# One weight array and one product of 448 columns for the second layer's queries and rotary keys

## The reference, cut to what matters

```python
def shared_kv(x, pos, kv_norm, kv_w_down, kv_latent_norm):
    h = rmsnorm(x, kv_norm)
    lat = h @ kv_w_down                     # 1024 -> 256 + 64
    ckv = rmsnorm(lat[..., :KV_LORA], kv_latent_norm)
    krope = rope(lat[..., KV_LORA:], pos)   # the rotary keys, 64 columns
    return ckv, krope
def mla_layer(x, k, v, pos, q_offset, norm_pre, w_in, q_norm, w_uq, w_out, norm_post):
    h = rmsnorm(x, norm_pre)
    proj = h @ w_in                         # 1024 -> 384 + 1024
    q_lat, gate = proj[..., :Q_LORA], proj[..., Q_LORA:]
    q = (rmsnorm(q_lat, q_norm) @ w_uq).reshape(B, T, H_B, NOPE + ROPE)
    ...
```

## Time and profile before

| | us |
|---|---|
| median of 3 runs | 659.3 |
| the runs | 660.23, 659.3, 653.32 |
| the profiled execution, its own time | 654.99 |
| its span, first to last instruction | 653.2 |
| PE busy | 619.9 (95%) |
| DVE busy | 401.2 (61%) |
| ACT busy | 297.5 (46%) |
| POOL busy | 123.7 (19%) |

### The profile page before, as it was taken

How to read it: one execution, slowest core, us unless ns; L and a number is a source line. 1 busy time by engine, 2 the same in 40 slices (tenths; PEclk the granted TensorE clock), 3 DMA queues, 4 the chain that set the end, 5 groups by cost and what they waited for, 6 DMA issues and landing times.

```text
span 653.2 us, 12063 instructions
## 1 busy us (share of the span) xinstructions
PE 619.9 (95%) x4702; PEld 598.4 (92%) x4702; DVE 401.2 (61%) x612; ACT 297.5 (46%) x578; POOL 123.7 (19%) x140
## 2 busy tenths in 40 slices
PE   5999999999999899997999999999999979989996
PEld 5989999999999799997999999988999978789996
DVE  5475755564564792258657767467788776664414
ACT  7785623432532352246323422365556667753311
POOL 0200200100030152236325400210000126630002
PEclk9999999999999899999999999999999999989999
DMA  8932280261262263232243410331111126766004
GB/s 317 332 108 65 64 259 18 66 204 55 74 193 66 73 228 112 83 112 98 67 113 84 129 65 2 112 85 30 34 29 38 49 81 199 236 214 255 1 1 162
DMA packets 66280, 73.68 MB, mean 113 GB/s; under 512 B 8112, under 2 KB 58544, under 8 KB 66096
## 3 DMA queue, kind: packets, MB, share of 16 engines
q1 hardware_dynamic: 66224, 72.91, 35.5%
HBM read 62.12 MB, written 10.78 MB: 112 GB/s over the span
## 4 chain that ended last, share of the span: by engine, by line
PE 64%; DVE 15%; ACT 11%; issue 4%; POOL 3%; DMA 3%; DVEq 0%; ACTq 0%; POOLq 0%
PE bank L1477 21%; PE bank L1479 20%; PE bank L1478 20%; DVE slab_lo L1175 2%; ACT prob L1109 2%; ACT slab_hi L922 2%; DVE pT_lo L1175 2%; DMA stage<-in_cache_ckv_dram 1%; DVE rows L1393 1%; DVE prob L1445 1%; DMA stage<-in_b_w_out_dram 1%; DVE qN_lo L1175 1%; DVE hat_lo L1175 1%; POOL skL L902 1%; POOL cn_lo L898 1%
## 5 line engine op out<-in xcount | busy, mean ns | idle before, releaser
L1477 PE MATMUL bank<-slab_hi,hat_hi 128*128 128x256 f32 (+2 forms) x600 | 171.8, 286 | 11.8 <-DVE slab_lo L1175 8.3
L1478 PE MATMUL bank<-slab_lo,hat_hi 128*128 128x256 f32 (+2 forms) x600 | 170.6, 284 | 0.0
L1479 PE MATMUL bank<-slab_hi,hat_lo 128*128 128x256 f32 (+2 forms) x600 | 170.5, 284 | 0.0
L1477 PEld LDWEIGHTS bank<-slab_hi,hat_hi 128*128 128x128 f32 x600 | 115.9, 193 | 12.7 <-DVE slab_lo L1175 8.5
L1478 PEld LDWEIGHTS bank<-slab_lo,hat_hi 128*128 128x128 f32 x600 | 116.0, 193 | 0.0
L1479 PEld LDWEIGHTS bank<-slab_hi,hat_lo 128*128 128x128 f32 x600 | 116.0, 193 | 0.0
L1175 DVE TENSOR_TENSOR slab_lo<-stage,slab_hi 128x1024 fp32r<-128x1024 f32 (+3 forms) x70 | 84.3, 1205 | 18.0 <-ACT slab_hi L922 16.0
L1477 PE MATMUL bank<-hat_hi,slab_hi 128*128 128x320 f32 x256 | 80.6, 315 | 0.6 <-DVE rows L1401 0.4
L1478 PE MATMUL bank<-hat_lo,slab_hi 128*128 128x320 f32 x256 | 79.8, 312 | 0.0
L1479 PE MATMUL bank<-hat_hi,slab_lo 128*128 128x320 f32 x256 | 79.7, 311 | 0.0
L922 ACT ACTIVATE slab_hi<-stage 128x1024 fp32r<-128x1024 f32 (+3 forms) x70 | 71.0, 1014 | 14.2 <-POOL stage L857 6.0
(11 more groups left out here) (334 smaller groups left out, 1440.5 us busy)
## 6 DMA issues: line engine op xcount, KB each, us to landing
stage<-in_a_w_in_dram SPq DMA_DIRECT2D x22, 512.0 KB, 5.1
stage<-in_b_w_in_dram SPq DMA_DIRECT2D x10, 512.0 KB, 4.2
st_s<-in_state_gla_dram SPq DMA_DIRECT2D x4, 1024.0 KB, 7.0
out_dram<-st_s SPq DMA_DIRECT2D x4, 1024.0 KB, 5.3
stage<-in_a_w_out_dram SPq DMA_DIRECT2D x8, 512.0 KB, 4.6
stage<-in_ckvT_dram SPq DMA_DIRECT2D x8, 512.0 KB, 3.5
stage<-in_cache_ckv_dram SPq DMA_DIRECT2D x8, 512.0 KB, 4.1
stage<-in_b_w_out_dram SPq DMA_DIRECT2D x8, 512.0 KB, 3.9
```

Source lines behind the costliest of these rows:

```text
L1477: pe.matmul(out, a[0], b[0], start=first, stop=False)
L1478: pe.matmul(out, a[0], b[1], start=False, stop=False)
L1479: return pe.matmul(out, a[1], b[0], start=False, stop=last)
```

## The change

`ql0` and `kq` become one weight `krq` of 448 columns (64 rotary, then 384 query). It has four pieces of two k-steps each, 896 elements a partition, in a slab of its own (slab 4), which lies where the second layer's latents and keys come later. Two pieces are loaded where `ql0` was, two where `kq` was. The products are one step for each tile, `("krq", t)`: 24 matmuls of 448 columns into one bank. PE waits before k-steps 0, 2, 4 and 6 of tile 0 for the pieces 0, 1, 2 and 3. DVE copies 64 and 384 columns out of each bank, and one step `kr` rotates the keys of all five tiles from the copy `kr_raw`. The other weights' alternation between slabs 0 and 1 leaves `krq` out.

```diff
-    out["ql0"] = halves("b_w_in", 0, "b_norm_pre")
-    out["kq"] = [[("kv_w_down", k, k + 4, KL, ROPE, "kv_norm"), ("b_w_in", k, k + 4, 256, QL - 256, "b_norm_pre")] for k in (0, 4)]
+    out["krq"] = [[("kv_w_down", k, k + 2, KL, ROPE, "kv_norm"), ("b_w_in", k, k + 2, 0, QL, "b_norm_pre")] for k in range(0, KD, 2)]
...
-SLAB_NO = {name: n for n, name in enumerate(SLABS)}
+SLAB_NO = {name: n for n, name in enumerate(name for name in SLABS if name != "krq")}
...
-            load("ql0")
+            out += [("piece", "krq", j) for j in range(2)]
...
 def latent_layer(out, load):
     out += [("lcn",)]
-    load("kq")
-    out += [("qa",), ("qas",)]
+    out += [("piece", "krq", j) for j in range(2, KD // 2)]
+    out += [("krq", t) for t in range(2)]
     load(("gb", 3))
-    out += [("kq",), ("kqs",), ("cn",), ("och",), ("qs",)]
+    out += [("krq", t) for t in range(2, NT)] + [("kr",), ("cn",), ("och",), ("qs",)]
...
         place[0] = qlT_at
+        slab[4] = pair("slab4", [P, KD * KRQ])
+        assert place[0] <= temp_at
+        kr_raw = thb[:, NT * ROPE:].rearrange("p (t n) -> p t n", n=ROPE)
+        place[0] = qlT_at
...
                 elif kind == "qs":
-                    after(pool, "act", "kqs")
+                    after(pool, "act", "krq", NT - 1)
                     s, r = S1(("qa",)), S1(("qa",), stat2)
-                    link(pool.tensor_tensor(r, s, S1(("qb",)), ADD))
-                    link(pool.tensor_scalar(r, r, 1.0 / QL, EPS, MUL, ADD))
+                    link(pool.tensor_scalar(r, s, 1.0 / QL, EPS, MUL, ADD))
...
+                    if name == "krq" and j == 0:
+                        after(act, "pe", "o", HA - 1)
+                        after(act, "dve", "gl", NT - 1)
+                        act.wait_ge(state_out, 16 * HA)
+                        act.wait_ge(final_out, 16 * HA)
...
+                elif kind == "krq":
+                    last = act.activation(junk[:, 0:QL], bank[:, 0, ROPE:KRQ], ACT.Square, accum_out=S1(("qa",), t=step[1]))
...
-                    if kind[0] == "q":
-                        last = dve.tensor_copy(qln[:, t, 0:256], v)
-                    else:
-                        link(rotate(krn[:, t, :], v[:, :, 0:ROPE],
-                                    [cst(c).rearrange("p (t n) -> p t n", n=RH)[:, t, :] for c in ("cos", "sin")], thb))
-                        last = dve.tensor_copy(qln[:, t, 256:QL], v[:, :, ROPE:ROPE + QL - 256])
+                elif kind == "krq":
+                    t = step[1]
+                    dve.tensor_copy(kr_raw[:, t, :], bank[:, 0, 0:ROPE])
+                    last = dve.tensor_copy(qln[:, t, :], bank[:, 0, ROPE:KRQ])
+                elif kind == "kr":
+                    last = rotate(krn, kr_raw, [cst(c).rearrange("p (t n) -> p t n", n=RH) for c in ("cos", "sin")], thb)
...
-                elif kind in ("qa", "qas"):
-                    last = natural(row, "ql0", range(NP) if kind == "qa" else [NP], 256, KD, hat)
-                elif kind in ("kq", "kqs"):
-                    last = natural(row, "kq", [NP] if kind == "kqs" else range(NP), ROPE + QL - 256, KD, hat)
+                elif kind == "krq":
+                    t = step[1]
+                    w = [x[:, 0:KD * KRQ].rearrange("p (k n) -> p k n", n=KRQ) for x in weights("krq")]
+                    for k in range(KD):
+                        if t == 0 and k % 2 == 0:
+                            after(pe, "dve", "piece", "krq", k // 2)
+                        last = mm3(bank[:, 0, 0:KRQ], cut(hat, A_, k, slice(t * P, (t + 1) * P)), cut(w, A_, k), k == 0, k == KD - 1)
```

More of the change, by code:

```diff
@@ L29 @@
 VG = DV + RANK
+KRQ = ROPE + QL
 Z_ORDER = (0, HA, 2, 3, 1)
@@ L86 @@
 SLABS = slabs()
-SLAB_NO = {name: n for n, name in enumerate(SLABS)}
+SLAB_NO = {name: n for n, name in enumerate(name for name in SLABS if name != "krq")}
 SLAB_AT = {name: n % 2 for name, n in SLAB_NO.items()}
 HALF_AT = {name: 0 for name in SLABS}
-SLAB_AT["v0g"] = 3
-PITCH = {name: 2 * VG if name == "v0g" else PIECE for name in SLABS}
+SLAB_AT["v0g"], SLAB_AT["krq"] = 3, 4
+PITCH = {name: {"v0g": 2 * VG, "krq": 2 * KRQ}.get(name, PIECE) for name in SLABS}
 for _g in range(2):
@@ L288 @@
     "rx": ("pool", "dve"), "lc": ("pe", "act", "dve"), "lcn": ("pool", "dve"), "gl": ("pe", "act", "dve"),
-    "cn": ("act", "dve"), "cT": ("pe", "act", "dve"), "qa": ("pe", "act", "dve"), "qas": ("pe", "act", "dve"),
-    "kq": ("pe", "act", "dve"), "kqs": ("pe", "act", "dve"), "qs": ("pool", "dve"), "gb": ("pe", "act", "dve"),
+    "cn": ("act", "dve"), "cT": ("pe", "act", "dve"), "krq": ("pe", "act", "dve"), "kr": ("dve",),
+    "qs": ("pool", "dve"), "gb": ("pe", "act", "dve"),
     "qT": ("pe", "act", "dve"), "qr": ("pe", "dve"), "qrT": ("pe", "act", "dve"), "qn": ("pe", "act", "dve"),
@@ L356 @@
 BANKED = [("vg", i) for i in range(3)] + [s for s in STEPS if "pe" in PARTS[s[0]] and s[0] != "vx"]
-ONE_BANK = ("z", "g0", "gl", "vs", "gts", "lc", "qT", "kh", "vh", "qabs", "O", "sv", "cx", "y0", "ys", "yt", "qas", "kqs", "os", "qr")
+ONE_BANK = ("z", "g0", "gl", "vs", "gts", "lc", "qT", "kh", "vh", "qabs", "O", "sv", "cx", "y0", "ys", "yt", "krq", "os", "qr")
 FIRST_BANKS = {("vg", 0): (0, 1), ("vg", 1): (2, 3), ("vg", 2): (4,), ("g0", 0): (5,), ("glT",): (6, 7), ("g0", 1): (0,),
@@ L384 @@
 BANK_NO, BANK_BEFORE = bank_numbers()
-USERS = {"v0g": ("vx", KD - 1), "kvc": ("lc", NT - 1), "ql0": ("qas",), "kq": ("kqs",), "uqr": ("qr", NT - 1), "uv": ("so",)}
+USERS = {"v0g": ("vx", KD - 1), "kvc": ("lc", NT - 1), "krq": ("krq", NT - 1), "uqr": ("qr", NT - 1), "uv": ("so",)}
 for _h in range(HA):
@@ L405 @@
         + [(("o", h), NT) for h in range(HA)] + [(("y", ph, t), 4) for ph in "AB" for t in range(NT)] \
-        + [(("yr", ph, t), 1) for ph in "AB" for t in range(NT)] + [(("lat",), NT), (("qa",), NT), (("qb",), NT)] \
+        + [(("yr", ph, t), 1) for ph in "AB" for t in range(NT)] + [(("lat",), NT), (("qa",), NT)] \
         + [(("S", h, u), 2) for h in range(HB) for u in range(2)] + [(("ss", b), 1) for b in range(SB)]:
@@ L689, in spot @@
             _w, k0, k1, _c0, cols, _g = SLABS[name][j][i]
-            if name == "kq":
+            if name == "krq":
                 wide = sum(w[4] for w in SLABS[name][j])
@@ L805, in _ @@
                     after(sp, "dve", "lcn")
-                    after(sp, "dve", "kqs")
+                    after(sp, "dve", "kr")
                     after(sp, "dve", "r", "A", NT - 1)
@@ L1087, in _ @@
                     _, s, j = step
-                    after(act, "dve", *(("gb", s, 0) if j else ("gb", s + 1, 1) if s < 3 else ("kqs",)))
+                    after(act, "dve", *(("gb", s, 0) if j else ("gb", s + 1, 1) if s < 3 else ("kr",)))
                     last = act.activation(thb[:, :].rearrange("p (a n) -> p a n", a=2), bank[:, :, 0:HALF], ACT.Tanh, scale=0.5)
@@ L1632, in _ @@
                     t = step[1]
-                    after(pe, "dve", "kqs")
+                    after(pe, "dve", "kr")
                     for c in range(KC):
```

## The result

The changed kernel is slower. Over 22 runs of each its median is 661.04 us against 655.0, and the ratio is **1.0107**, with a 95% interval of 1.0085 to 1.0128. The medians lie 6.0 us apart and the ratio makes 7.0 us of 655.0, where 6.6 were forecast; the time lies inside the range of 657 to 668. The loss is clear of noise but small, on the line of about 1% that the prediction drew between slower and the same. (The median of before is now lower than the 659.3 of its first three runs.)

What follows compares the result with a forecast made beforehand. PE was taken to bound the kernel, busy 95% of the span. Terms -3.8 + 8.9 + 2.1 - 1.5 + 0.9 gave +6.6 us: 661.6 on the profiled 655.0, 664.2 on the runs' mean; put at 662.5, range 657 to 668.

Steps and rivals of the forecast that it cites:

- The order of the reading: Profile page, PE's timeline, then DVE and POOL: both `kq` pieces ready only at 331.81, 12 us after `qa` began.
- Its length: PE's wait for piece 2 in tile 0 of `krq`, wanted at 322.2, ready about 331.1: +8.9 us (8.0 to 9.5).
- The product: `krq` stream on PE: 120 matmuls of 448 columns at 0.200 us replace 240, -3.8 us (3.6 to 4.0 saved).
- The rival of cost by columns alone: `krq` product: merging saves nothing, 448 columns take 0.2315 us, sum +10.4, 665.4 us; chance 0.04.
- The half clock: Behind the wait for piece 2, PE's granted clock drops for a while: +2.1 us, bounds 0 and 3.2.
- The kind case: Rival at the wait: clock stays or returns at once, or all terms end kindly; +3 to +5, 658 to 660; chance 0.24.
- In front and behind: From `rx` 4, DVE gets through earlier, -1.5 us; after the product, PE waits on DVE's `gb` and `cT` readings, +0.9.
- The cover of the first `cT`: Behind the product: `kr` ends by T + 7.0, just before `cT` needs it at T + 7.05; T is the product's end.
- The five terms: Across the changed stretch: product -3.8, wait +8.9, clock +2.1, in front -1.5, behind +0.9; sum +6.6 us.

Runs made afterwards that it cites:

- the run with late ("gb", 3) gains: The changed kernel, with POOL waiting for PE's first `krq` tile before the gains of ("gb", 3): 658.25 us, ratio 1.0046.
- the split run: The changed kernel with pieces 2 and 3 early and each tile's product made as two, 256 and 192 columns: 654.86 us, ratio 0.9985.
- late `uqr` gains: The changed kernel with pieces 2 and 3 early, ("gb", 2) gains behind `qs`, and `uqr` gains behind the second ("gb", 2) low half: 652.53 us, ratio 0.9971.
- the run with work in the wait: The changed kernel, with PE repeating k-steps 0 to 3 of tile 0 three more times before the real ones: 659.08 us, ratio 1.0072.

## Why the prediction was right, step by step

**The order of the reading carried it.** The forecast did not rest on the product, which is a gain in every run, but on what the old product had covered. `qa` had 14.4 us of work on a weight that was there; tile 0 of `krq` has 2.4 us before it needs the third of four pieces. Placing the pieces early takes the ratio from 1.0107 to 0.9942. This is shown.

**Its length.** 8.9 us were worked out; 9.2 were lost, 9.05 of them idle. POOL's six gains took 8.2 us (321.26 to 329.47), where 7.6 to 8.1 had been reckoned. The rule behind it, one DVE instruction for each POOL instruction, is seen in the ends of the six pairs above and borne out by two experiments in opposite places: fewer POOL instructions cut the wait to 5.83 us, and a short one in the kernel before cut PE's wait from 1.90 to 0.64. The Trainium skill (GPSIMD Engine Reference, Specifications) says that GpSimd shares its SBUF interfaces with VectorE and names two SBUF inputs and the two-port modes as the cases that clash. The runs agree: the `lcn` scalings and low halves read two inputs from SBUF and were held, whereas a `krq` copy out of PSUM (at 332.29 in the run with late ("gb", 3) gains) took its usual 0.55 us beside a gain that ran from 331.55. The scaling of `rx` 4 was held as well, 2.41 us against 0.76, though it reads one tensor; so two inputs are not needed for it, and whether it ran in a two-port mode no row shows.

**The product was mis-sized.** The term was -3.8; it is -3.05 in the profiled pair and -3.4 where the wait is gone. The slope from 320 to 512 columns gave 0.200 us for 448. The stream ran at 0.206 in the profiled execution of the changed kernel and at 0.203 in the five others with 448 columns, also in the two where the wait was still there; so it is not the wait that makes the difference, and -3.4 is the better figure. Why 0.203 is above the line, and what made 0.206 of it in one execution, stays open. The rival of cost by columns alone is excluded by the split run. The Trainium skill's rule for an isolated matmul (TensorE: Matmul & The Clock Gate, Back-to-back issue gap), columns over 2.4 plus 2.5 ns, is no price for these products: estimated by it, 224 columns take 95.8 ns and 448 take 189.2, where the runs show 112 and 203 to 206. The same section says that in a stream of weight loads and matmuls the rule counts too little at few columns and too much at many; the runs agree with the first and not with the second.

**The half clock** was put at 2.1 us, with bounds 0 and 3.2; it was 2.8 in the profiled execution. The kind case, a clock that stays up through a short idle time, is not to be counted on: it fell around 1.76 us as well. The length of the idle time did not decide it in the trace of the kernel before either, which the prediction had read only in part: there the clock stayed at 1.00 through 2.83 us (533.55) and was 0.50 for 3.4 us from about 576.4, behind an idle time of 1.69.

**In front and behind** came out within 0.2 us of the forecast (-1.49 for -1.5, +0.76 for +0.9). The cover of the first `cT` held: its matmuls start at 362.62, right behind the first `gb`, and DVE ends `kr` at 360.70, T + 5.1. I had put that at T + 7.0 with no margin. One `kr` instruction was caught by POOL's gains, not two.

**What the agreement of the totals is worth.** The five terms come to 8.26 us in the traces against 6.6; product and clock were both too kind by 0.7. The profiled execution of the changed kernel took 4.1 us more than its median, and the medians lie only 6.0 us apart. The 662.5 that was put on record had been set between two readings of three runs of before; on the median of 22, 655.0, the sum would have given 661.6. So the mechanism and the wait were foreseen, but that the total came within 1.5 us is partly luck.

**The rest of the 10.16 us** of the profiled pair is no part of the change. The time behind ("gb", 2, 0) is 290.3 us in the changed kernel, 289.0 before, 286.8 with early pieces and 290.3 with late `uqr` gains. In the two slowest the granted clock was 0.50 for most of a stretch of ten microseconds in the sample stage, and in the other two it was not, although PE idles there for 2.7 to 2.8 us in each. The kernel before has the 3.4 us at half clock from 576.4 in this part, and the run with early pieces has none, so the times go in the order of the time at half clock. PE's idle time and the window of the changed kernel in that stage, and then those of before:

```profile
542.40 0.76 PE L1476 MATMUL bank<-sT_hi,qab_hi 128*128 128x512 f32 x1 [2.73 <-POOL skL L905]
541.00:551.00 10.00, 8.60 (x28) 7.57 (x29) 4.89 (x5) 5.44 (x8) 5.54 (x3) 0.52 0.51 147
```

```profile
533.55 0.47 PE L1477 MATMUL bank<-sT_hi,qab_hi 128*128 128x512 f32 x1 [2.83 <-POOL skL L902]
532.00:543.00 11.00, 9.45 (x61) 8.59 (x62) 8.12 (x9) 8.94 (x13) 5.94 (x4) 1.00 0.55 154
```

The runs of the changed kernel show the same spread: 657.67 us at a mean clock of 0.990, 667.38 at 0.972. What decides it in one execution was not tried.

## What to carry to other kernels

When small products are merged into a wider one, look at what the first of the old ones covered: a weight that was needed in halves is needed whole in the first tile. Here moving two pieces in the order of steps turned a loss of 1.1% into a gain of 0.6%. Not all of that needs the merger: the kernel before with one short first gain stands at 0.9959, not to be told in time from 0.9942. And count what POOL does beside DVE in instructions, not in busy time: where DVE works from SBUF into SBUF, its next instruction came through when POOL's current one ended. Two gains fewer in the wait cut it by 3.2 us, and one shorter gain in front was worth 1.3.

## What the runs showed of the hardware that was not expected

- Matmuls of these rounded halves, each with a weight load of its own (PE and PEld both count 4702 in the kernel before), have a least distance of about 0.112 us: 0.1115 at 192 columns and 0.112 at 224. At 256 it is 0.120, at 448 0.203 to 0.206.
- The granted clock fell to 0.50 around a PE idle time of 1.76 us in the run with work in the wait, and stayed at 1.00 through 2.83 us in the kernel before; in the same place of the changed kernel it fell around 2.73 us.
- Splitting one POOL instruction of 1024 elements into 256 and 768 took 1.3 us off PE's path in the trace; the whole kernel came out at 0.9959 (0.9924 to 0.9994).
